# First attention layer of a two-block transformer kernel: token tile 1 ahead of tile 0, share copies ahead of the next scores, and the last output products in another order

## The chip, the cores and the metric

The kernel runs on one core of one Trainium2 chip. The metric is the device time of one execution in microseconds; lower is better. Times of the trace are microseconds from the start of its span.

## The reference, cut to what matters

Two transformer blocks over 256 tokens of width 1024. The part that the change touches is the attention layer of the first block, with the norm behind it:

```
k, v = split(rms_norm(x, kv_norm) @ w_kv)          # 16 heads of 64
q    = rms_norm(x, b_norm) @ w_q
sc   = q_c @ k_c.T * 64**-0.5 + bias[clip(i - j)]  # per chunk of 64 queries, keys of this and the chunks to its left
x    = x + (softmax(sc) @ v) @ w_o
x    = x + (silu(g) * u) @ w_down    with g, u = split(rms_norm(x, ffn_norm) @ w_gate_up)
```

Ahead of it stand a gated mixer and a feed-forward layer; behind it feed-forward 1, and then the second block with its own feed-forwards, sparse and stick-breaking attention and a memory attention.

## The kernel before, in words

The program is written out by hand, engine by engine; the order of the calls in each engine's function is the order in which that engine works, and semaphores join the engines. The 256 tokens are two tiles t of 128 rows.

Every weight matrix is cut into units of 1 MB. SyncE (SP, L562) loads unit u into one of three slots `raw`, once VectorE has split unit u-3. `split_to(n)` on ScalarE (ACT, L730) rounds it into `w_hi` and on VectorE (DVE, L1054) writes the rest into `w_lo`; these are rings of four, so ACT waits until TensorE (PE) has used unit u-4 (`s_used`). `product` (L1663 to L1665) is three matmuls, high by high, high by low and low by high. The units here are `U_KQ` to `U_KQ+7` (keys and queries in turn, 256 columns each), `U_O` to `U_O+3` (output projection) and then, as `U_O+4` and up, gate and up of feed-forward 1.

PSUM holds four accumulators `acc` and four banks `turn`. `take(n)` gives bank n % 4 and waits until VectorE has freed the use before it (`s_tfree`). The numbers are dealt out ahead (`N_S1`, `N_P1`, `T_O`) and must follow the order of the calls on PE and DVE.

The attention runs in six steps (`STEPS1`): for each group g of eight heads, tile 0 with all heads (128 keys) and tile 1 in two steps of four heads (256 keys). A step i is

- `scores(i)` on PE (L1825), into two banks;
- `shift(i)` on DVE: scale and bias (L1209), row maximum (L1212), its negative (L1213), for each half;
- `exps(i)` on ACT (L838): the exponentials, in place in `sc`;
- `turn_shares(i)` on PE (`turn`, L1656): eight transposes into two banks;
- `shares(i)` on DVE: two copies `pt` (L1141);
- `values(i)` on PE (L1845), shares by values, into `acc[2t+1]`.

After the last step of a tile and group come `heads_out(t, g)` on DVE (`xn`, L1229), `turn_heads_out` on PE (four transposes), `high_out` on ACT (L748) and `low_out` on DVE (L1064). `out_tile(t, half, g)` on PE is 12 matmuls of 512 columns of the output projection: eight such tiles, of which (t, half, 0) starts an accumulator and (t, half, 1) ends it. `kq_tile(i, e)` is half a unit of keys or queries, 24 matmuls of 256 columns; `read_kq(i)` on ACT (L829) copies the result to `kt` or `qt`. `read_values(b)` (L821) reads the value block b.

Behind the last output products stand `residual` (L1097), `gained` (`xn`, L1085) and `turn_rows` of the norm, then `by_columns_start`: 48 products of tile 0 of the tokens with the first four gate and up units (i = 0 to 3) and 48 of tile 1, with a hook that turns the second tile's rows ahead of (t=0, i=3).

Of the kernel before, what the change touches and what calls it, by code (L numbers as in the profile page):

```python
# [7 lines left out]
P = 128  # L8
# [4 lines left out]
ACT = mybir.ActivationFunctionType  # L13
# [59 lines left out]
def build(nc, ins, out):  # L73
# [149 lines left out]
    for gp in range(5):  # L223
        if gp < 4:
            MIX_ORDER += [("mix", gp, 0), ("mix", gp, 1)]
        if gp >= 1:
# [15 lines left out]
              for t, js in ((0, (0, 1, 2, 3)), (1, (0, 1)), (1, (2, 3)))]  # L242
    N_S1, N_P1, T_O = [banks(2)], [], {}
    for i in range(6):
        N_P1.append(banks(2))
        if i == 4:
            N_S1.append(banks(2))
            T_O[0, 1] = splits(1)
        elif i < 5:
            N_S1.append(banks(2))  # L250
            if i in (1, 3):
                T_O[(0, 0) if i == 1 else (1, 0)] = splits(1)
        else:
            T_O[1, 1] = splits(1)
# [59 lines left out]
    with ExitStack() as ctx:  # L314
# [405 lines left out]
        def _(act):  # L720
# [104 lines left out]
            def read_kq(i):  # L825

                act.wait_ge(s_used, U_KQ + i + 1)
                dst = (kt_, qt)[i % 2][:, 2 * (i // 2):2 * (i // 2) + 2, :].rearrange("p k n -> p (k n)")
                nc.scalar.activation(dst, acc[2 * (i % 2)][:], ACT.Copy).then_inc(s_kq, 1)  # L829
# [22 lines left out]
            for i in range(4):  # L852
                read_kq(i)
                split_to(U_KQ + 5 + i)
            exps(0)
            read_kq(4)
            split_to(U_O + 1)
            exps(1)
            read_kq(5)
            split_to(U_O + 2)  # L860
            exps(2)
            read_kq(6)
            split_to(U_O + 3)
# [3 lines left out]
            exps(3)  # L867
            exps(4)
            high_out(1, 0)
            exps(5)  # L870
            high_out(0, 1)
            squares(R_FFN1, 0, X, s_row, 3, squares_out[:])
            high_out(1, 1)
            split_to(U_O + 6)
            high_rows(F[1]["norm"], 0, 0)
            split_to(U_O + 7)
            squares(R_FFN1, 1, X, s_read, C_O + 2, squares_out[:])
            split_to(U_O + 8)
            high_rows(F[1]["norm"], 0, 1)
            ffn(1)  # L880
# [158 lines left out]
        def _(dve):  # L1039
# [183 lines left out]
            def heads_out(t, g):  # L1223

                rs = rs1[:, t, 8 * g:8 * g + 8]
                dve.wait_ge(s_exp, 2 * (3 * g + 2 * t + 1))
                link(V.reciprocal(rs, sum1[:, t, 8 * g:8 * g + 8]))
                dve.wait_ge(s_pv, 2 * (3 * g + 2 * t + 1))
# [10 lines left out]
            split_to(U_KQ + 8)  # L1239
            dve.wait_ge(s_rel, 1)  # L1240
            shift(0)
            shares(0)
            shift(1)
            split_to(U_O + 1)
            heads_out(0, 0)
            shares(1)
            shift(2)
            split_to(U_O + 2)
            low_out(0, 0)
            split_to(U_O + 3)  # L1250
            shares(2)
            shift(3)
            heads_out(1, 0)
            split_to(U_O + 4)
            shares(3)
            shift(4)
            low_out(1, 0)
            heads_out(0, 1)
            shares(4)
            shift(5)  # L1260
            low_out(0, 1)
            shares(5)
            residual(2, C_O, U_O + 3, 0)
            heads_out(1, 1)
            gained(G_FFN1, 0, s_row, 3)
            low_out(1, 1)
            split_to(U_O + 6)
            low_rows(F[1]["norm"], 0, 0)
            residual(2, C_O, U_O + 3, 1)
            split_to(U_O + 7)  # L1270
            gained(G_FFN1, 1, s_read, C_O + 2)
            split_to(U_O + 8)
# [371 lines left out]
        def _(pe):  # L1644
# [42 lines left out]
            def by_columns_start(u0, c, src, tr, hooks={}):  # L1687

                for t in range(TT):
                    tok = slice(t * P, (t + 1) * P)  # L1690
                    pe.wait_ge(*freed(tr[t][0] + 1))
                    for i in range(4):
# [7 lines left out]
                        for k in range(4):  # L1700
                            last = product(acc[2 * (b % 2) + t][:], [src(hl, k0 + k)[:, tok] for hl in range(2)],
                                           weights(u, k, BLK), k0 + k == 0, k0 + k == KD - 1)
# [52 lines left out]
            def ffn(f, g, tail, hooks={}):  # L1755
# [7 lines left out]
                by_columns_start(u0, c0, xt_hl(0), F[f]["norm"], {(0, 3): lambda: turn_rows(F[f]["norm"], g, 1), **hooks})  # L1763
# [71 lines left out]
            def values(i):  # L1835
                g, t, js = STEPS1[i]
                nk = keys_of(t)
                if g == 1 and i % 3 < 2:
                    pe.wait_ge(s_o, t + 1)
# [27 lines left out]
            for i in range(4):  # L1867
                if i == 1:
                    pe.wait_ge(*freed(T_Q[1][0] + 1))
                for e in range(2):  # L1870
                    kq_tile(i, e)
            kq_tile(4, 0)
            scores(0)
            kq_tile(4, 1)
            kq_tile(5, 0)
            turn_shares(0)
            scores(1)
            kq_tile(5, 1)
            values(0)
            kq_tile(6, 0)  # L1880
            turn_shares(1)
            scores(2)
            kq_tile(6, 1)
            values(1)
            turn_heads_out(0, 0, 1)
# [411 lines left out]
```

## Time and profile before

| | |
|---|---|
| median of 3 runs | 1272.08 us (1270.84 to 1272.70) |
| the profiled execution, device time | 1273.68 us |
| its span, first to last instruction | 1271.9 us |
| its mean granted TensorE clock | 0.981 of 2.4 GHz |

The span is what the trace sees; 1.8 us of the execution's own time lie around it. Shares of busy time are over the whole span. A timeline row is the start, the duration, the engine, the line, what is written and read and, in brackets, how long the engine had been idle and who released it.

### The profile page before, as it was taken

What the parts mean: (1) busy time and instruction counts of PE and PEld (TensorE: products, weight loads), DVE (VectorE), ACT (ScalarE), POOL (GpSimd) and SP (SyncE); (2) the same over time, 40 slices, a digit from 0 to 9 for tenths busy, and PEclk for the clock granted to TensorE, in tenths of its full rate; (3) what the DMA queues carried; (4) which work ended last, traced back from release to release, by engine and by line L of the source; (5) the groups of instructions that cost most, each with busy time, mean ns of one, the idle gap of its engine ahead of it and who ended that gap; (6) DMA issues with size and microseconds to landing.
All of it is one profiled execution on the core that took longest, in us unless ns stands there. A gap on an engine that the chain in (4) does not pass through costs nothing.

```text
span 1271.9 us, 14904 instructions
## 1 busy us (share of the span) xinstructions
PE 1227.4 (97%) x6231; PEld 1027.6 (81%) x6231; DVE 702.8 (55%) x707; ACT 552.1 (43%) x652; POOL 67.5 (5%) x121
## 2 busy tenths in 40 slices
PE   5998999999999989999998999999999997999998
PEld 4886888888889977888886888888988876888886
DVE  4567356545375655655535555535944677554552
ACT  4444254444355524544524534424555324444341
POOL 4000010000010001010001000003200011000000
PEclk9998999999999979999999999999999897999999
DMA  8752546556486315675554655554752223456550
GB/s 281 254 196 83 196 149 213 184 198 205 160 265 220 112 34 184 199 231 182 207 174 149 198 190 176 205 191 128 230 168 83 84 83 100 155 178 197 199 198 33
DMA packets 147825, 218.46 MB, mean 172 GB/s; under 512 B 5136, under 2 KB 115760, under 8 KB 147632
## 3 DMA queue, kind: packets, MB, share of 16 engines
q1 hardware_dynamic: 144640, 206.69, 49.3%
q0 software_dynamic: 3120, 10.84, 2.6%
q8 instruction: 49, 0.80, 0.3%
q14 instruction: 16, 0.13, 0.0%
HBM read 216.45 MB, written 1.05 MB: 171 GB/s over the span
## 4 chain that ended last, share of the span: by engine, by line
PE 91%; DVE 5%; ACT 1%; issue 1%; DMA 1%; POOL 0%; SPq 0%; DVEq 0%; POOLq 0%; ACTq 0%
PE acc L1663 28%; PE acc L1665 27%; PE acc L1664 27%; PE turn L1656 4%; DVE w_lo L1054 1%; DVE xt L1064 1%; DMA raw<-in_a_w_in 1%; ACT w_hi L730 1%; PE acc L2087 1%; PE turn L2065 1%; PE acc L1845 1%; PE turn L1951 1%; PE turn L1825 1%; DVE pt L1141 0%; PE turn L2036 0%
## 5 line engine op out<-in xcount | busy, mean ns | idle before, releaser
L1054 DVE TENSOR_TENSOR w_lo<-raw,w_hi 128x2048 fp32r<-128x2048 f32 (+1 forms) x196 | 442.4, 2280 | 207.5 <-ACT w_hi L730 207.2
L1663 PE MATMUL acc<-w_hi,xt 128*128 128x512 f32 (+2 forms) x1112 | 438.1, 394 | 13.6 <-DVE xt L1064 9.5
L730 ACT ACTIVATE w_hi<-raw 128x2048 fp32r<-128x2048 f32 (+1 forms) x196 | 368.0, 1906 | 148.4 <-PE acc L1665 117.5
L1665 PE MATMUL acc<-w_hi,xt 128*128 128x512 f32 (+2 forms) x1112 | 430.7, 387 | 0.0
L1664 PE MATMUL acc<-w_lo,xt 128*128 128x512 f32 (+2 forms) x1112 | 430.4, 387 | 0.0
L1663 PEld LDWEIGHTS acc<-w_hi,xt 128*128 128x128 f32 x1112 | 211.5, 190 | 57.8 <-DVE xt L1064 11.8
L1665 PEld LDWEIGHTS acc<-w_hi,xt 128*128 128x128 f32 x1112 | 211.4, 190 | 43.0
L1664 PEld LDWEIGHTS acc<-w_lo,xt 128*128 128x128 f32 x1112 | 211.9, 191 | 40.0
L775 ACT ACTIVATE sg<-acc,rstd 128x256 f32<-128x256 f32 x88 | 37.0, 472 | 246.8 <-PE acc L1665 246.8
L1663 PE MATMUL acc<-w_hi,ht 128*128 128x512 f32 x352 | 139.6, 397 | 0.0
L1665 PE MATMUL acc<-w_hi,ht 128*128 128x512 f32 x352 | 138.0, 392 | 0.0
L1664 PE MATMUL acc<-w_lo,ht 128*128 128x512 f32 x352 | 136.6, 388 | 0.0
L1125 DVE SCALAR_TENSOR_TENSOR hh<-acc,rstd,sg 128x256 f32<-128x256 f32 x88 | 38.5, 479 | 177.1 <-ACT sg L775 177.1
L1665 PEld LDWEIGHTS acc<-w_hi,ht 128*128 128x128 f32 x352 | 66.1, 188 | 15.4
L1664 PEld LDWEIGHTS acc<-w_lo,ht 128*128 128x128 f32 x352 | 66.1, 188 | 14.3
L1663 PEld LDWEIGHTS acc<-w_hi,ht 128*128 128x128 f32 x352 | 66.2, 188 | 12.8
L748 ACT ACTIVATE xt<-turn 128x512 fp32r<-128x512 f32 x54 | 29.7, 597 | 63.5 <-PE turn L1656 63.5
L1663 PE MATMUL acc<-xt,w_hi 128*128 128x256 f32 x192 | 55.1, 287 | 1.3 <-ACT val L821 1.3
L1664 PE MATMUL acc<-xt,w_hi 128*128 128x256 f32 x192 | 54.3, 283 | 0.0
L1665 PE MATMUL acc<-xt,w_lo 128*128 128x256 f32 x192 | 54.3, 283 | 0.0
L615 POOL TENSOR_SCALAR ss<-ss 128x1 f32<-128x1 f32 (+1 forms) x21 | 9.2, 439 | 808.7 <-ACT xn L739 492.6
L1064 DVE TENSOR_TENSOR xt<-turn,xt 128x512 fp32r<-128x512 f32 x54 | 35.0, 685 | 19.2 <-ACT xt L748 18.9
(257 smaller groups left out, 868.8 us busy)
## 6 DMA issues: line engine op xcount, KB each, us to landing
raw<-in_ffn_w_gate_up SPq DMA_DIRECT2D x88, 512.0 KB, 5.1
raw<-in_ffn_w_down SPq DMA_DIRECT2D x22, 1024.0 KB, 5.0
raw<-in_ffn_wg SPq DMA_DIRECT2D x44, 512.0 KB, 4.1
raw<-in_ffn_wu SPq DMA_DIRECT2D x44, 512.0 KB, 5.2
raw<-in_ffn_wd SPq DMA_DIRECT2D x22, 1024.0 KB, 5.1
raw<-in_a_w_in SPq DMA_DIRECT2D x16, 1024.0 KB, 6.0
raw<-in_w_in SPq DMA_DIRECT2D x10, 1024.0 KB, 5.4
raw<-in_a_w_out SPq DMA_DIRECT2D x8, 1024.0 KB, 5.2
```

What stands on the lines that cost most here:

```text
L730: nc.scalar.activation(w_hi[:, u % RING, 0:kt * w], raw[:, u % RAW, 0:kt * w], ACT.Copy).then_inc(s_hi, 1)
L748: nc.scalar.activation(dst, src, ACT.Copy).then_inc(s_thi, 1)
L775: nc.scalar.activation(sg[:, b % 2, t, :], acc[2 * ((c0 + b) % 2) + t][:, 0:FFN_BLK], ACT.Silu, scale=rstd[:, R_FFN[f], t:t + 1]).then_inc ...
L1054: V.tensor_tensor(w_lo[:, u % RING, 0:kt * w], raw[:, u % RAW, 0:kt * w], w_hi[:, u % RING, 0:kt * w].bitcast(F32), ALU.subtract).then_inc ...
L1064: V.tensor_tensor(dst, src, hi.bitcast(F32), ALU.subtract).then_inc(s_tfree, 1)
L1125: last = V.scalar_tensor_tensor(hh[:, b % 2, t, :], acc[2 * ((c0 + b) % 2) + t][:, FFN_BLK:2 * FFN_BLK], rstd[:, R_FFN[f], t:t + 1], sg[:, ...
L1656: last = nc.tensor.transpose(b[:, i * P:(i + 1) * P], src, ident[:])
L1663: mm(o, lhs[0], rhs[0], start=start, stop=False)
L1664: mm(o, lhs[0], rhs[1], start=False, stop=False)
L1665: return mm(o, lhs[1], rhs[0], start=False, stop=stop)
L1825: last = mm(banks2[half][:, e * nk:(e + 1) * nk], qt[rows, j, t * P:(t + 1) * P], kt_[rows, j, 0:nk], start=True, stop=True)
L1845: last = mm(acc[2 * t + 1][:, (h % 8) * HEAD:(h % 8 + 1) * HEAD], pt1[:, half, e * nk + kk * P:e * nk + (kk + 1) * P], val[:, kk, h * HEAD ...
```

## The change

`STEPS1` now has, for each group, tile 1 with its first four heads, tile 1 with its last four, and then tile 0. The accumulators of keys and queries are swapped: the first (keys) is `acc[2]`, so that the first `kq_tile` waits only for value block 0. Scores of step 0 and 3 wait for two reads of keys and queries less, since they need only the first half of a group; step 0 moves up between the halves of `kq_tile` 2. On DVE `shares(i)` stands ahead of `shift(i+1)`, with `shift(4)` and `shift(5)` next to each other. The end is rewritten: which output product stands between which attention parts, `squares` of ACT behind the high copies, and the hook of feed-forward 1 two products later (`late`). The computation is the same.

```
     STEPS1 = [(g, t, [4 * g + j for j in js]) for g in range(2)
-              for t, js in ((0, (0, 1, 2, 3)), (1, (0, 1)), (1, (2, 3)))]
+              for t, js in ((1, (0, 1)), (1, (2, 3)), (0, (0, 1, 2, 3)))]
...
-                        pe.wait_ge(s_read, C_V + 2)
+                        pe.wait_ge(s_read, C_V + 1 + i)
...
-                    last = product(acc[2 * (i % 2)][:, e * TOK:(e + 1) * TOK], weights(u, k, 256, e * P, P),
+                    last = product(acc[2 - 2 * (i % 2)][:, e * TOK:(e + 1) * TOK], weights(u, k, 256, e * P, P),
...
-                pe.wait_ge(s_kq, 4 * (g + 1))
+                pe.wait_ge(s_kq, 4 * (g + 1) - 2 * (i % 3 == 0))
...
-            def out_tile(t, half, g):
+            def out_tile(t, half, g, between=None):
 
                 for k in range(4 * g, 4 * g + 4):
                     u = U_O + k // 2
+                    if k % 4 == 2 and between:
+                        between()
...
-                    if (t, half) == (1, 1 - C_O % 2) and k % 2 == 1:
+                    if (t, half) == (1, C_O % 2) and k % 2 == 1:
                         last.then_inc(s_used, 1)
...
+            kq_tile(2, 0)
+            scores(0)
+            kq_tile(2, 1)
+            kq_tile(3, 0)
+            turn_shares(0)
+            kq_tile(3, 1)
+            values(0)
             kq_tile(4, 0)
-            scores(0)
+            scores(1)
...
             kq_tile(7, 0)
+            turn_shares(3)
+            turn_heads_out(0, 0, 2)
             kq_tile(7, 1)
-            turn_shares(2)
+            values(3)
+            scores(4)
             pe.wait_ge(*freed(T_O[0, 0][0]))
             pe.wait_ge(s_kq, 8)
-            out_tile(0, 0, 0)
-            scores(3)
-            values(2)
-            out_tile(0, 1, 0)
-            turn_shares(3)
-            scores(4)
-            turn_heads_out(1, 0, 2)
-            values(3)
+            near, far = C_O % 2, 1 - C_O % 2
+            out_tile(0, far, 0, lambda: scores(5))
+            out_tile(0, near, 0)
             turn_shares(4)
-            scores(5)
-            turn_heads_out(0, 1, 3)
             values(4)
+            turn_shares(5)
+            pe.wait_ge(s_o, 3)
+            out_tile(1, far, 0)
+            turn_heads_out(1, 1, 3)
+            values(5)
+            pe.wait_ge(*freed(T_O[1, 1][0]))
+            out_tile(1, far, 1, lambda: turn_heads_out(0, 1, 4))
             pe.wait_ge(*freed(T_O[0, 1][0]))
-            out_tile(0, 0, 1)
-            out_tile(0, 1, 1).then_inc(s_half, 1)
-            turn_shares(5)
-            out_tile(1, C_O % 2, 0)
-            values(5)
-            pe.wait_ge(s_o, 4)
-            out_tile(1, 1 - C_O % 2, 0)
-            turn_heads_out(1, 1, 4)
-            pe.wait_ge(*freed(T_O[1, 1][0]))
-            out_tile(1, C_O % 2, 1)
+            out_tile(0, near, 1)
+            out_tile(0, far, 1).then_inc(s_half, 1)
+            out_tile(1, near, 0)
             turn_rows(F[1]["norm"], G_FFN1, 0)
-            out_tile(1, 1 - C_O % 2, 1)
-            ffn(1, G_FFN1, lambda: turn_rows(F[2]["norm"], G_FFN2, 0))
+            out_tile(1, near, 1)
+            ffn(1, G_FFN1, lambda: turn_rows(F[2]["norm"], G_FFN2, 0), late=True)
```

`C_O` is 25, so `near` is half 1 (`acc[0]`, `acc[1]`) and `far` is half 0 (`acc[2]`, `acc[3]`).

What this makes of the order, at two places. On PE before, from the transposes of step 3's shares to the first product of the second group; `sc` are shares, `kt,qt` scores, `xn` head outputs and `val,pt` values:

```order
1908 L1656 MATMUL turn<-ident,sc 128x128 x8
1909 L1825 MATMUL turn<-kt,qt 128x256 x4
1910 L1656 MATMUL turn<-ident,xn 128x128 x4
1911 L1845 MATMUL acc<-val,pt 128x64 x8
1912 L1656 MATMUL turn<-ident,sc 128x128 x8
1913 L1825 MATMUL turn<-kt,qt 128x256 x4
1914 L1656 MATMUL turn<-ident,xn 128x128 x4
1915 L1845 MATMUL acc<-val,pt 128x64 x8
1916 L1663 MATMUL acc<-w_hi,xt 128x512
```

On PE of the change, from `values(3)` to `scores(5)` inside the output tile (its lines stand some numbers lower in the file: L1664 is `turn`, L1836 scores, L1856 values, L1671 to L1673 the product):

```order
1886 L1856 MATMUL acc<-val,pt 128x64 x8
1887 L1836 MATMUL turn<-kt,qt 128x256 x4
1888 L1671 MATMUL acc<-w_hi,xt 128x512
1889 L1672 MATMUL acc<-w_lo,xt 128x512
1890 L1673 MATMUL acc<-w_hi,xt 128x512
1891 L1671 MATMUL acc<-w_hi,xt 128x512
1892 L1672 MATMUL acc<-w_lo,xt 128x512
1893 L1673 MATMUL acc<-w_hi,xt 128x512
1894 L1836 MATMUL turn<-kt,qt 128x128 x8
```

and 18 matmuls of output products later, around `values(4)`:

```order
1913 L1664 MATMUL turn<-ident,sc 128x128 x8
1914 L1856 MATMUL acc<-val,pt 128x64 x8
1915 L1664 MATMUL turn<-ident,sc 128x128 x8
1916 L1671 MATMUL acc<-w_hi,xt 128x512
1917 L1672 MATMUL acc<-w_lo,xt 128x512
```

Before, eight attention groups stand in a row; now both last scores stand ahead of output products, and between two output tiles only three groups are left.

On DVE before, from the shift of step 5 to the norm (`sc` the shift, `pt` the share copies, `X` the residual, `xn<-X` the gain, `xt` the low copies):

```order
157 L1212 TENSOR_REDUCE mx<-sc 128x2
158 L1213 TENSOR_SCALAR nm<-mx 128x2
159 L1064 TENSOR_TENSOR xt<-turn,xt 128x4x128
160 L1141 COPY pt<-turn 128x512 x2
161 L1097 TENSOR_TENSOR X<-acc,X 128x512 x2
162 L1227 RECIPROCAL rs<-sum 128x8
163 L1229 TENSOR_TENSOR xn<-acc,rs 128x512
164 L1085 TENSOR_TENSOR xn<-X,gain_rows 128x1024
165 L1064 TENSOR_TENSOR xt<-turn,xt 128x4x128
166 L1054 TENSOR_TENSOR w_lo<-raw,w_hi 128x2048 x2
167 L1064 TENSOR_TENSOR xt<-turn,xt 128x4x128 x2
```

On DVE of the change, from the copies of step 4 to the low copies of the norm's first tile:

```order
156 L1148 COPY pt<-turn 128x512 x2
157 L1234 RECIPROCAL rs<-sum 128x8
158 L1236 TENSOR_TENSOR xn<-acc,rs 128x512
159 L1148 COPY pt<-turn 128x512 x2
160 L1061 TENSOR_TENSOR w_lo<-raw,w_hi 128x2048
161 L1071 TENSOR_TENSOR xt<-turn,xt 128x4x128
162 L1234 RECIPROCAL rs<-sum 128x8
163 L1236 TENSOR_TENSOR xn<-acc,rs 128x512
164 L1071 TENSOR_TENSOR xt<-turn,xt 128x4x128
165 L1104 TENSOR_TENSOR X<-acc,X 128x512 x2
166 L1092 TENSOR_TENSOR xn<-X,gain_rows 128x1024
167 L1061 TENSOR_TENSOR w_lo<-raw,w_hi 128x2048
```

The weight split of `U_O+3` moved behind the copies of step 5, both head outputs now come ahead of the residual, and one weight split of feed-forward 1 comes ahead of the low copies of the norm.

## Rows read from the trace of the kernel before

**Rows 1.** The page, busy time and share of each engine
```profile
PE 1227.4 (97%) x6231; PEld 1027.6 (81%) x6231; DVE 702.8 (55%) x707; ACT 552.1 (43%) x652; POOL 67.5 (5%) x121
```
**Rows 2.** PE's timeline, the rows of the attention stage behind idle time
```profile
381.93 0.36 PE L1663 MATMUL acc<-xt,w_hi 128*128 128x256 f32 x1 [1.27 <-ACT val L821]
...
449.44 0.63 PE L1656 MATMUL turn<-ident,xn 128*128 128x128 f32 x4 [0.25 <-DVE pt L1141]
...
452.60 0.66 PE L1656 MATMUL turn<-ident,sc 128*128 128x128 f32 x4 [0.79 <-ACT sc L838]
...
454.12 0.92 PE L1656 MATMUL turn<-ident,sc 128*128 128x128 f32 x4 [0.86 <-ACT sc L838]
455.41 2.08 PE L1825 MATMUL turn<-kt,qt 64*128 64x256 f32 x8 [0.38 <-DVE xt L1064]
...
463.01 0.80 PE L1663 MATMUL acc<-w_hi,xt 128*128 128x512 f32 x1 [1.16 <-DVE xt L1064]
...
477.33 0.50 PE L1663 MATMUL acc<-w_hi,xt 128*128 128x512 f32 x1 [0.85 <-DVE xn L1229]
...
482.24 0.50 PE L1663 MATMUL acc<-w_hi,xt 128*128 128x512 f32 x1 [1.41 <-DVE xt L1064]
...
489.05 0.50 PE L1663 MATMUL acc<-w_hi,xt 128*128 128x512 f32 x1 [0.15 <-DVE xt L1064]
```
**Rows 3.** Windows: length, busy time by engine, granted clock (PEclk), DMA share, GB/s
```profile
408.00:448.00 40.00, 40.00 (x325) 37.16 (x324) 28.08 (x40) 21.43 (x58) 0.00 (x0) 1.00 0.34 112
454.40:468.00 13.60, 12.06 (x44) 9.67 (x43) 6.37 (x12) 2.81 (x10) 0.00 (x0) 0.50 0.01 1
...
977.00:982.00 5.00, 5.00 (x45) 4.52 (x44) 2.43 (x6) 0.69 (x1) 0.00 (x0) 1.00 0.02 3
997.00:1007.40 10.40, 10.40 (x51) 9.39 (x51) 6.34 (x12) 3.79 (x9) 0.00 (x0) 0.51 0.58 202
```
**Rows 4.** The chain that ended last: start, duration, engine and line
```profile
408.06 1.09 PE turn L1825 x16
...
415.11 0.87 PE turn L1656 x8
...
420.11 1.73 PE acc L1845 x16
...
431.50 0.44 PE turn L1656 x4
...
487.80 1.21 DVE xt L1064 x2
```
**Rows 5.** PE's timeline: a product behind the norm's transposes, and block 0's end
```profile
498.14 0.47 PE L1663 MATMUL acc<-w_hi,xt 128*128 128x512 f32 x1
...
511.88 0.38 PE L1656 MATMUL turn<-ident,hh 128*128 128x128 f32 x2
```
**Rows 6.** DVE's timeline: shifts, share copies, the splits ahead of feed-forward 1
```profile
409.86 0.68 DVE L1209 SCALAR_TENSOR_TENSOR sc<-turn,rel 128x512 f32<-128x512 f32 x1
...
415.58 1.29 DVE L1141 COPY pt<-turn 128x512 f32<-128x512 f32 x2 [2.60 <-PE turn L1656]
417.08 0.69 DVE L1209 SCALAR_TENSOR_TENSOR sc<-turn,rel 128x512 f32<-128x512 f32 x1 [0.20 <-PE turn L1825]
...
420.04 0.17 DVE L1213 TENSOR_SCALAR nm<-mx 128x2 f32<-128x2 f32 x1
...
483.30 4.50 DVE L1054 TENSOR_TENSOR w_lo<-raw,w_hi 128x2048 fp32r<-128x2048 f32 x2 [1.11 <-ACT w_hi L730]
```
**Rows 7.** ACT's timeline: ends of two steps' exponentials, weights ahead of feed-forward 1
```profile
414.52 0.19 ACT L838 ACTIVATION_READ_ACCUMULATOR sc<-sc,nm 128x1 f32 x1
...
421.15 0.19 ACT L838 ACTIVATION_READ_ACCUMULATOR sc<-sc,nm 128x1 f32 x1
...
481.36 3.71 ACT L730 ACTIVATE w_hi<-raw 128x2048 fp32r<-128x2048 f32 x2
...
492.05 1.92 ACT L730 ACTIVATE w_hi<-raw 128x2048 fp32r<-128x2048 f32 x1 [0.65 <-DMA raw<-in_ffn_w_gate_up]
```

More of the change, by code:

```diff
@@ L241, in build @@
     STEPS1 = [(g, t, [4 * g + j for j in js]) for g in range(2)
-              for t, js in ((0, (0, 1, 2, 3)), (1, (0, 1)), (1, (2, 3)))]
-    N_S1, N_P1, T_O = [banks(2)], [], {}
-    for i in range(6):
+              for t, js in ((1, (0, 1)), (1, (2, 3)), (0, (0, 1, 2, 3)))]
+    N_S1, N_P1, T_O = [], [], {}
+    for i in range(3):
+        N_S1.append(banks(2))
         N_P1.append(banks(2))
[L246 to L254, printed above, removed]
+    N_S1.append(banks(2))
+    T_O[1, 0] = splits(1)
+    N_P1.append(banks(2))
+    T_O[0, 0] = splits(1)
+    for i in (4, 5):
+        N_S1.append(banks(2))
+    for i in (4, 5):
+        N_P1.append(banks(2))
+    T_O[1, 1] = splits(1)
+    T_O[0, 1] = splits(1)
     C_O = blocks(2)
@@ L828, in read_kq @@
                 dst = (kt_, qt)[i % 2][:, 2 * (i // 2):2 * (i // 2) + 2, :].rearrange("p k n -> p (k n)")
-                nc.scalar.activation(dst, acc[2 * (i % 2)][:], ACT.Copy).then_inc(s_kq, 1)
+                nc.scalar.activation(dst, acc[2 - 2 * (i % 2)][:], ACT.Copy).then_inc(s_kq, 1)
             def exps(i):
@@ L851, in _ @@
             split_to(U_KQ + 4)
-            for i in range(4):
-                read_kq(i)
-                split_to(U_KQ + 5 + i)
+            read_kq(0)
+            split_to(U_KQ + 5)
+            read_kq(1)
+            split_to(U_KQ + 6)
             exps(0)
+            read_kq(2)
+            split_to(U_KQ + 7)
+            read_kq(3)
+            split_to(U_KQ + 8)
+            exps(1)
             read_kq(4)
             split_to(U_O + 1)
-            exps(1)
+            exps(2)
             read_kq(5)
             split_to(U_O + 2)
-            exps(2)
+            exps(3)
             read_kq(6)
+            high_out(1, 0)
             split_to(U_O + 3)
@@ L866, in _ @@
             split_to(U_O + 4)
-            exps(3)
             exps(4)
-            high_out(1, 0)
             exps(5)
+            high_out(1, 1)
             high_out(0, 1)
+            split_to(U_O + 5)
+            high_rows(F[1]["norm"], 0, 0)
+            split_to(U_O + 6)
             squares(R_FFN1, 0, X, s_row, 3, squares_out[:])
[L873 to L877, printed above, removed]
             split_to(U_O + 8)
             high_rows(F[1]["norm"], 0, 1)
+            squares(R_FFN1, 1, X, s_read, C_O + 2, squares_out[:])
             ffn(1)
@@ L1242, in _ @@
             shares(0)
+            split_to(U_KQ + 8)
             shift(1)
[L1244 to L1245 removed]
             shares(1)
             shift(2)
[L1248 to L1250 removed]
+            split_to(U_O + 1)
+            heads_out(1, 0)
             shares(2)
             shift(3)
[L1253 removed]
+            split_to(U_O + 2)
+            heads_out(0, 0)
+            low_out(1, 0)
+            shares(3)
+            split_to(U_O + 3)
+            low_out(0, 0)
+            shift(4)
+            shift(5)
+            shares(4)
+            heads_out(1, 1)
+            shares(5)
             split_to(U_O + 4)
[L1255 to L1257 removed]
+            low_out(1, 1)
             heads_out(0, 1)
[L1259 to L1260 removed]
             low_out(0, 1)
[L1262 removed]
             residual(2, C_O, U_O + 3, 0)
[L1264 removed]
             gained(G_FFN1, 0, s_row, 3)
[L1266 removed]
+            split_to(U_O + 5)
+            low_rows(F[1]["norm"], 0, 0)
             split_to(U_O + 6)
[L1268 removed]
             residual(2, C_O, U_O + 3, 1)
[L1270 removed]
+            split_to(U_O + 8)
             gained(G_FFN1, 1, s_read, C_O + 2)
[L1272 removed]
             low_rows(F[1]["norm"], 0, 1)
@@ L1753, in turn_rows, with ffn @@
                     turn(tr[t][0] + q, [xn[:, t, k * P:(k + 1) * P] for k in range(4 * q, 4 * q + 4)])
-            def ffn(f, g, tail, hooks={}):
+            def ffn(f, g, tail, hooks={}, late=False):
                 (u0, ud), c0 = U_FFN[f], F[f]["c"]
@@ L1866, in _ @@
                                                         (1, 2): lambda: [turn_rows(T_Q, G_B, t) for t in range(TT)]})
[L1867 to L1871, printed above, removed]
+            for e in range(2):
+                kq_tile(0, e)
+            pe.wait_ge(*freed(T_Q[1][0] + 1))
+            for e in range(2):
+                kq_tile(1, e)
+            kq_tile(2, 0)
@@ L1872, in _ @@
+            scores(0)
[4 more added lines that the diff above has]
+            values(0)
             kq_tile(4, 0)
-            scores(0)
+            scores(1)
             kq_tile(4, 1)
             kq_tile(5, 0)
[L1876 to L1880, printed above, removed]
             turn_shares(1)
             scores(2)
+            kq_tile(5, 1)
+            values(1)
```

22 lines of the change are left out of this document (14 added, 8 removed).

## The prediction

> **What bounds the kernel now.** I read the page first: PE is busy 1227.4 us of the span [rows 1], so what can be won is PE's idle time and the time that it spends at the lower clock. The waits and then PE's timeline of the attention stage show where it idles [rows 2]: once ahead of the first keys (1.27 us, for ACT's copies of the values), and then eight times between 449 and 489 us: 0.25, 0.79, 0.86, 0.38, 1.16, 0.85, 1.41 and 0.15, together 5.85 us. The releasers are ACT's exponentials and DVE's copies, so what ends last there is a round trip PE, DVE, ACT, DVE, PE with nothing on PE to cover it. The windows show the second loss [rows 3]: up to 448 us PE is busy throughout at a granted clock of 1.00 (2.4 GHz), although scores, transposes and values are mixed into the keys and queries there; from 454.4 to 468.0 it is 0.50 (1.2 GHz), with PE busy 12.06 us. It fell right behind the waits of 0.79 and 0.86 us.
>
> The Trainium skill (TensorE: Matmul & The Clock Gate, "HAM oscillation — how this bites in real kernels") ties the fall to one long idle gap. The trace does not agree: no gap ahead of this fall is longer than 0.86 us. By the page alone I would not count a fall in the new order; below I keep one as a rival.
>
> **What the change gives back.** All amounts of PE work stay: 16 halves of keys and queries at 2.90 us (nine from 381.93 to 408.06 [rows 2, 4]), six scores at 1.09, six transposes of shares at 0.87 to 0.96, six values at 1.73, four transposes of heads at 0.44 [rows 4], eight output tiles at 2.75 (60 matmuls of 512 columns in 511.88 - 498.14 = 13.74 us, so 12 in 2.75 [rows 5]). SP, POOL and the number of DMAs stay too. Only covers change.
>
> 1. *First keys.* `acc[2]` is read out with value block 0, one block ahead of the read that PE waits for, so the 1.27 us come back.
>
> 2. *Exponentials.* From the start of a shift to the end of the exponentials it takes 421.34 - 417.08 = 4.3 us for tile 1 and 414.71 - 409.86 = 4.9 us for tile 0 [rows 6, 7]. Before, step 4's had little more than what stands between 449.44 and 452.60 to hide in [rows 2]. In the new order: step 0's scores end about 1 us before DVE is free of a weight split, so they need 5.3 us and have two key halves, 5.8: 0.5 spare, the thinnest. Steps 1 to 3 have one or two halves, values and transposes: 1.5 to 3.7 spare. Step 4 has an output tile and a half or more plus `scores(5)`: 1.5 + 1.1 + 1.5 + 2.75 = 6.85 against 4.3. Step 5's shift starts behind step 4's, which takes 420.21 - 417.08 = 3.1, so its exponentials end 3.1 + 4.9 = 8.0 us after the scores of 4, and are wanted at 6.85 + 0.95 + 0.45 + 1.75 = 10.0. Both waits (0.79, 0.86) go.
>
> 3. *Head outputs and their low copies.* The way turn, ACT, DVE, PE left PE idle for 1.41 us with nothing on it [rows 2]. Now `values(5)` (1.73) stands behind the turn of (1,1), and half an output tile (1.5) behind the turn of (0,1): both just enough. The 0.85 behind `values(5)` lies under half an output tile; that of `values(4)` under the transposes of step 5 (0.9 against 0.85). The waits 0.25, 0.38, 1.16, 0.85, 1.41 go, within 0.1 each.
>
> 4. *Clock.* With the waits gone PE has an output tile on either side of a stretch of about 4 us (transposes, values, transposes). A like mix held 1.00 from 977 to 982 us with PE busy throughout [rows 3]. If the clock holds, 12.06 us of busy time at half clock become 6.0: 6.0 us back.
>
> 5. *Drains.* A wait costs a little more than its idle row, since the last matmul's end overlaps nothing. I put 0.1 on each of the eight waits, 0.8, an estimate: it is what the walk below gives beyond the other terms.
>
> Back: 1.27 + 5.85 + 6.0 + 0.8 = 13.9 us.
>
> **What it costs.**
>
> a. `values(4)` now directly follows its transposes. The first copy starts 0.47 us behind the first transpose (415.58 against 415.11) and takes half of 1.29, so it ends at 1.12, the second at 1.76 [rows 4, 6]; PE is done with its transposes after 0.87 to 0.96 and waits for the first copy and, if at all, a little for the second: 0.4 us.
>
> b. *Start of feed-forward 1.* `U_O` is released in `out_tile(1, near, 0)`, one product pair into the third tile from the end; PE then has 1.4 + 0.87 + 2.85, about 4.9 us with latencies, left. In that time ACT rounds `U_O+4` (1.86, half of 3.71), DVE splits it (2.25, half of 4.50) and, now behind it, makes the low copies of the norm (1.21) [rows 4, 6, 7]: 5.4. PE waits 0.5, against 0.15 before (already taken as given back). Then the splits of `U_O+5` and `+6` with the residual between them end some 5.7 us after the start, where PE has 5.6 of work: 0.15. `U_O+7` is loaded only when `U_O+4` is split. Before, that split ended at 485.6 and the rounding, released by the DMA, began at 492.05: 6.5 us [rows 6, 7]. So rounding starts 6.5 us behind the split, or 5 if the load alone is quicker; with 1.86 and 2.25 behind it PE waits 0 to 0.95 us. The hook, two products later, leaves 1.4 us of products behind its transposes, for a high copy on ACT and DVE's 1.21 of low copies, some 1.7 to 1.8 from the transposes' end: 0.25 or a little more. Together 0.9 to 1.85; middle 1.4.
>
> c. *Breaks.* Each change from one kind of matmul to products costs about 0.1, an estimate. Two split output tiles and more, smaller pieces among the keys: three breaks more, 0.3.
>
> d. At nothing: `squares` of tile 1 behind the high copies (1.1 us later; its rstd is wanted by the first Silu, 5 us on; without that cover 1.1). `U_O+3` is split behind the copies of step 5; in the walk its product comes 3 us after that, and ACT wants the load behind it 15 us later. In all halves of keys and queries the split is ready over 2 us ahead.
>
> Costs 0.4 + 1.4 + 0.3 = 2.1. Net 13.9 - 2.1 = 11.8 us. As a check I walked PE's new order from 380.6 with these durations: the 48 products of tile 1 end between 499.4 and 500.3 us, against 511.88, so 11.6 to 12.5. From there on the order is as before and PE-bound, so nothing should take it back. The profiled execution's 1273.68 becomes 1261.9; it lies 1.6 above the median of the runs, so the forecast for the median is 1272.08 - 11.8 = 1260.3.
>
> **Rivals.**
>
> *The clock falls again (0.18).* For: it fell behind waits of under a microsecond, and the new tail has one of 0.4 us amid attention groups. Against: before, eight groups in a row and six waits; the stretch at 977. Price: up to the 6.0 of term 4, so 1266.3; half that if it falls for half as long. The Trainium skill (same page, "A second HAM failure mode: psum-queue depth-cycling") says that small idles between groups of matmuls cycling through PSUM banks can make the clock go to and fro, which speaks against an order with more such groups. By it the sum would be this rival's; the trace agrees for 454 us and not for 408 to 448.
>
> *Thin covers fail (0.11).* Step 0's exponentials, the low copies, the splits of feed-forward 1: three places with under 0.5 us spare, each late by a microsecond: 1263.3.
>
> *The waits only move (0.04).* Every wait on DVE turns up at the next consumer, and the clock falls as before: 1271, within 0.2%.
>
> *Slower (0.05).* Scores and values now start 13 us earlier (395 instead of 408), so more of the stage is a mix. If PE went to 1.2 GHz in it early and stayed there, it would cost half of that time: 23.6 us at 1.2 GHz undo the 11.8; 30 us give 1275.5. For: falls last long here (13.6 us; 10.4 at 997 us [rows 3]). Against: the same mix held 1.00 for the 40 us up to 448 us.
>
> **How the numbers follow.** The forecast case has 0.62, with a range of its own of 1258.3 to 1262.5: the bounds of b (0.5 each way), the drains (0.8), and the low stretches further on, which may begin or end a little otherwise when everything ahead of them is 12 us earlier (10.4 us at half clock is worth 5; I allow 1.5 either way). The range of 8 in 10 reaches up over both middle rivals to 1266.5; below there is no more to win than the 0.9 to 1.85 of b, so 1258.0. Faster by over 0.2% (2.5 us, about what a measurement of this kernel can tell): 0.91; within it 0.04; slower 0.05.
>
> **What the changed profile would show.** PE's first key product without idle ahead of it; the granted clock 1.00 from 381 to 500 us; no row of PE waiting for ACT's `sc`; one wait of about 0.4 us for `pt` around 452; one of about 0.5 us at the first gate and up product around 476, and perhaps one for `w_lo` at 484; the first `hh` transpose near 500 instead of 511.88; the rest of the trace shifted by 12 us. I am wrong if the clock shows 0.50 around 450 to 465, if PE waits for `sc` around 402, or if the gain at 500 us is given back later.

## The result, and the profile after

The changed kernel takes 1260.64 us (median of 4 runs, 1259.60 to 1262.52) against 1272.22 us (4 runs, 1270.84 to 1272.70): a ratio of 0.9911 with a 95% interval of 0.9899 to 0.9924, 11.6 us faster. The forecast was 1260.3. The profiled execution took 1260.18 us, with a span of 1258.5 us and a mean granted clock of 0.989. Two executions far outside all the others, 2049.05 us for the kernel before and 2442.75 us for a variant further down, are left out of what follows.

The page's first line for the changed kernel: PE has the same 6231 matmuls and is 7.3 us less busy than in [rows 1]; the other engines are as before.

```profile
PE 1220.1 (97%) x6231; PEld 1022.9 (81%) x6231; DVE 702.5 (56%) x707; ACT 551.9 (44%) x652; POOL 66.9 (5%) x121
```

PE's timeline, with the last 16 transposes ahead of the stage, the change from the last value product to the first key product, all the rows with idle time between 379 and 499 us, two product rows around a wait of the weight loads, and the first transpose of feed-forward 1:

```profile
372.26 1.91 PE L1664 MATMUL turn<-ident,xn 128*128 128x128 f32 x16
...
379.24 0.39 PE L1673 MATMUL acc<-w_hi,xt 128*128 128x512 f32 x1
379.46 0.28 PE L1671 MATMUL acc<-xt,w_hi 128*128 128x256 f32 x1
...
451.44 2.00 PE L1856 MATMUL acc<-val,pt 128*128 128x64 f32 x16 [0.41 <-DVE pt L1148]
...
475.49 0.51 PE L1671 MATMUL acc<-w_hi,xt 128*128 128x512 f32 x1 [0.46 <-DVE xt L1071]
...
483.72 0.39 PE L1673 MATMUL acc<-w_hi,xt 128*128 128x512 f32 x1
484.22 0.51 PE L1671 MATMUL acc<-w_hi,xt 128*128 128x512 f32 x1
...
488.35 0.50 PE L1671 MATMUL acc<-w_hi,xt 128*128 128x512 f32 x1 [0.18 <-DVE xt L1071]
...
499.36 0.60 PE L1664 MATMUL turn<-ident,hh 128*128 128x128 f32 x4
```

Products of 512 columns otherwise start 0.23 us apart; the two at 483.72 and 484.22 are 0.50 apart, since the second waits for `w_lo`.

Nine waits [rows 2] have become three. The first key product follows the last value product at once; no row waits for ACT's `sc`. The windows of the changed kernel (length; PE, PEld, DVE, ACT and POOL busy; granted clock; DMA share; GB/s), first those that answer to [rows 3], then everything ahead of the stage, the stage from the 16 transposes to the first `hh` transpose, and everything behind it:

```profile
408.00:448.00 40.00, 40.00 (x332) 37.19 (x332) 28.38 (x44) 20.32 (x51) 0.00 (x0) 1.00 0.36 120
454.40:468.00 13.60, 13.58 (x71) 11.20 (x72) 5.42 (x7) 1.20 (x2) 0.00 (x0) 1.00 0.25 77
...
0.00:372.26 372.26, 355.30 (x1596) 293.43 (x1597) 201.47 (x174) 158.80 (x146) 26.59 (x52) 0.99 0.59 198
372.26:499.36 127.10, 125.91 (x857) 111.89 (x856) 79.87 (x94) 64.45 (x113) 7.04 (x10) 1.00 0.48 154
499.36:1258.50 759.14, 738.91 (x3780) 617.56 (x3778) 421.12 (x441) 328.68 (x393) 33.26 (x59) 0.99 0.50 165
```

The same three parts of the kernel before:

```profile
0.00:373.30 373.30, 355.88 (x1597) 293.24 (x1597) 201.57 (x174) 158.83 (x146) 27.37 (x52) 0.99 0.59 197
373.30:511.88 138.58, 131.45 (x858) 116.59 (x857) 79.91 (x94) 64.48 (x113) 7.01 (x10) 0.95 0.44 142
511.88:1271.90 760.02, 740.07 (x3780) 617.81 (x3778) 421.29 (x441) 328.81 (x393) 33.11 (x59) 0.98 0.50 165
```

The stage went from 138.58 to 127.10 us, 11.48 less; that is nearly all of the 11.6 us between the medians. The two profiled spans differ by 13.4: 1.04 more ahead of the stage and 0.88 more behind it, where the program is the same. Those parts vary from one execution to the next (behind the stage 756.9 to 761.5 us over the kernels below, with low-clock stretches of other lengths), so from here on I read the stage's length. It tells kernels apart that the whole time does not.

### The profile page after: what moved, and what is told of

It reads as the page before. It is cut to its first block, busy times and chain, and to the rows that moved or that the text cites. A ratio compares the mean times of both kernels' runs of the same rounds, so it can differ in the third digit from the quotient of the medians.

```text
span 1258.5 us, 14904 instructions
## 1 busy us (share of the span) xinstructions
PE 1220.1 (97%) x6231; PEld 1022.9 (81%) x6231; DVE 702.5 (56%) x707; ACT 551.9 (44%) x652; POOL 66.9 (5%) x121
## 4 chain that ended last, share of the span: by engine, by line
PE 91%; DVE 4%; ACT 2%; DMA 1%; issue 1%; POOL 0%; SPq 0%; DVEq 0%; ACTq 0%; POOLq 0%
PE acc L1671 28%; PE acc L1673 27%; PE acc L1672 27%; PE turn L1664 4%; DVE w_lo L1061 1%; ACT w_hi L732 1%; PE acc L1856 1%; PE acc L2103 1%; DVE xt L1071 1%; DMA raw<-in_a_w_in 1%; PE turn L2081 1%; PE turn L1967 1%; PE turn L1836 1%; DMA raw<-in_ffn_w_gate_up 0%; PE turn L1986 0%
## 5 line engine op out<-in xcount | busy, mean ns | idle before, releaser
L1671 PE MATMUL acc<-w_hi,xt 128*128 128x512 f32 (+2 forms) x1112 | 438.0, 394 | 10.5 <-DVE xt L1071 6.8
L1673 PE MATMUL acc<-w_hi,xt 128*128 128x512 f32 (+2 forms) x1112 | 430.3, 387 | 0.0
L1671 PEld LDWEIGHTS acc<-w_hi,xt 128*128 128x128 f32 x1112 | 211.3, 190 | 55.5 <-DVE xt L1071 9.5
L1673 PEld LDWEIGHTS acc<-w_hi,xt 128*128 128x128 f32 x1112 | 210.8, 190 | 42.8
L1671 PE MATMUL acc<-w_hi,ht 128*128 128x512 f32 x352 | 139.7, 397 | 0.0
L1673 PE MATMUL acc<-w_hi,ht 128*128 128x512 f32 x352 | 138.1, 392 | 0.0
L1673 PEld LDWEIGHTS acc<-w_hi,ht 128*128 128x128 f32 x352 | 66.1, 188 | 15.4
L1671 PEld LDWEIGHTS acc<-w_hi,ht 128*128 128x128 f32 x352 | 66.3, 188 | 12.8
L1671 PE MATMUL acc<-xt,w_hi 128*128 128x256 f32 x192 | 55.5, 289 | 0.0
L1673 PE MATMUL acc<-xt,w_lo 128*128 128x256 f32 x192 | 54.3, 283 | 0.0
L1071 DVE TENSOR_TENSOR xt<-turn,xt 128x512 fp32r<-128x512 f32 x54 | 35.0, 684 | 13.5 <-ACT xt L750 13.4
```

The lines of the kernel that those rows point to most:

```text
L1071: V.tensor_tensor(dst, src, hi.bitcast(F32), ALU.subtract).then_inc(s_tfree, 1)
L1671: mm(o, lhs[0], rhs[0], start=start, stop=False)
L1673: return mm(o, lhs[1], rhs[0], start=False, stop=stop)
```

## Experiments

In all of them "stage" is the time from the 16 transposes to the first `hh` transpose: 138.58 us before, 127.10 changed. Kernels are compared with runs of the kernel before on the same chip.

### The accumulators of keys and queries as before

```diff
-   acc[2 - 2 * (i % 2)][:], ACT.Copy)
+   acc[2 * (i % 2)][:], ACT.Copy)
...
-   pe.wait_ge(s_read, C_V + 1 + i)
+   pe.wait_ge(s_read, C_V + 2)
```

The same swap of `acc` stands in `product`. 

> The changed kernel with only the swap of the key and query accumulators undone (keys in acc[0], first key product behind both value reads). If the first-keys term stands by itself, PE idles 1.3 us again ahead of the first key product and the time is 1.3 us above the changed kernel's 1260.6: about 1261.9. If the wait was hidden by something further on, it stays at 1260.6.

Measured: 1265.11 us, ratio 0.9945 (0.9932 to 0.9959), stage 129.14. PE's timeline has the old wait back, to the hundredth:

```profile
381.51 0.36 PE L1671 MATMUL acc<-xt,w_hi 128*128 128x256 f32 x1 [1.27 <-ACT val L823]
```

The stage lost 2.04 us, not 1.3; the rest is a wait of 0.66 us for `w_lo` in feed-forward 1, of which more below. The time is 3.2 us above the expected 1261.9, and 4.5 above the changed kernel's median, more than the stage shows. Its profiled execution was one of its faster ones (1263.26 us; all six lie between 1263.22 and 1267.81): of the 3.0 us between its span (1261.5) and that of the changed kernel, 2.04 lie in the stage and the rest where the program is the same. What the median has beyond that, no trace shows.

### The new steps, but the output products in a row at the end

```diff
-   out_tile(0, far, 0, lambda: scores(5))
-   out_tile(0, near, 0)
+   scores(5)
    turn_shares(4)
    values(4)
    turn_shares(5)
-   out_tile(1, far, 0)
    turn_heads_out(1, 1, 3)
    values(5)
-   out_tile(1, far, 1, lambda: turn_heads_out(0, 1, 4))
+   turn_heads_out(0, 1, 4)
+   out_tile(0, far, 0); out_tile(0, near, 0)
+   out_tile(1, far, 0); out_tile(1, far, 1)
```

The waits between these calls are left out of the diff; the order on DVE and ACT is that of the changed kernel.

> The changed kernel with the output products of group 0 taken out from between the last attention parts: scores 5, shares 4, values 4, shares 5, values 5 and both head transposes stand in a row behind scores 4, and the output tiles follow. Step order, first keys, DVE and ACT stay as changed. If the output products are the cover, PE waits about 3.3 us for step 4's exponentials, about 1 us for its copies, and some more; 4 to 5 us of idle in all, and the clock falls behind it as before, 3 to 6 us more: 1268 to 1271. If idle alone counts and the clock holds: 1265. If the order of the steps alone gives the gain, products or no products between: 1261.

Measured: 1271.23 us, ratio 0.9995 (0.9984 to 1.0005), stage 137.48. All but 1.1 us of the stage's gain is gone. The first keys' wait is still absent, which alone is worth about that much. The tail in PE's timeline:

```profile
446.07 0.66 PE L1664 MATMUL turn<-ident,sc 128*128 128x128 f32 x4 [1.94 <-ACT sc L840]
447.59 0.66 PE L1664 MATMUL turn<-ident,sc 128*128 128x128 f32 x4 [0.86 <-ACT sc L840]
450.09 3.67 PE L1856 MATMUL acc<-val,pt 128*128 128x64 f32 x16 [1.85 <-DVE pt L1148]
...
459.96 1.11 PE L1664 MATMUL turn<-ident,xn 128*128 128x128 f32 x4 [1.95 <-DVE xn L1236]
```

The values of step 4 last 3.67 us, those of the changed kernel 2.00: the clock fell, as the windows of the same kernel say.

```profile
449.30:456.10 6.80, 6.01 (x28) 6.01 (x29) 3.35 (x7) 1.85 (x10) 0.00 (x0) 0.50 0.00 0
459.50:462.90 3.40, 2.94 (x9) 2.55 (x10) 1.10 (x2) 0.60 (x1) 0.00 (x0) 0.50 0.95 298
```

So the order of the steps and the copies ahead of the next scores, as they stand, win nothing further without the output products between them.

### One cover moved: `scores(5)` behind both output tiles

```diff
-   out_tile(0, far, 0, lambda: scores(5))
+   out_tile(0, far, 0)
    out_tile(0, near, 0)
+   scores(5)
```

> The changed kernel with scores 5 behind the two output tiles of token tile 0 instead of inside the first. Shift 5 starts some 4 us later, so the exponentials of step 5 end 1.5 to 2.5 us after PE wants them. Cover theory: that idle and no more if the clock holds: 1262.5; with a fall of the clock behind the wait up to 6 us on top, 1264 to 1268.5. Rival: the place of scores 5 doesn't matter, 1260.6.

Measured: 1267.12 us, ratio 0.9961 (0.9948 to 0.9973), stage 133.30, that is 6.2 us lost by moving 1.1 us of work. Up to the first gate and up product the stage lost 5.26 us (481.37 - 372.88 = 108.49 against 475.49 - 372.26 = 103.23); the other 0.94 lie behind it, where this trace has a wait of 1.02 us for `w_lo`. PE's timeline, and the windows of the same kernel:

```profile
454.35 3.68 PE L1856 MATMUL acc<-val,pt 128*128 128x64 f32 x16 [2.80 <-DVE pt L1148]
```

```profile
449.00:454.40 5.40, 2.60 (x27) 1.89 (x26) 3.70 (x8) 2.18 (x11) 0.00 (x0) 1.00 0.01 3
454.40:461.20 6.80, 6.80 (x28) 6.46 (x29) 3.34 (x6) 1.00 (x6) 0.00 (x0) 0.50 0.00 0
```

It was one wait, for `pt` and not for `sc` as I had expected: the copies of step 4 now stand on DVE behind the shift of step 5, which stands behind the late scores. The wait grew from 0.41 to 2.80, and with it the clock fell for 6.8 us.

### The same with PE kept at work in the wait

Nine more matmuls of 512 columns go into a free bank ahead of `values(4)`, and are overwritten there; the output is unchanged.

```diff
    scores(5)
    turn_shares(4)
+   for _ in range(9):
+       mm(take(N_P1[5])[:], xt[0][:, 0, 0, 0:P], w_hi[:, U_O % RING, 0:BLK], start=True, stop=True)
```

> The kernel with scores 5 late, with nine extra matmuls of 512 columns in its wait of 2.80 us ahead of values 4; they are overwritten, no output changes. That kernel's stage was 133.3 us, 6.2 above the changed one's, with the clock at 0.50 for 6.8 us. If the wait makes the clock fall, it now holds 1.00 and the stage is 129.9 to 130.5: the wait alone costs 2.4 to 3, the clock 3 to 3.4. If the clock falls for another reason, the stage stays at 133.3 or grows.

Measured: 1265.34 us, ratio 0.9938 (0.9922 to 0.9954), stage 129.78. PE's timeline, and the window of the same kernel that fell before:

```profile
450.51 2.33 PE L1920 MATMUL turn<-w_hi,xt 128*128 128x512 f32 x9
453.55 2.00 PE L1856 MATMUL acc<-val,pt 128*128 128x64 f32 x16 [0.71 <-DVE pt L1148]
```

```profile
454.40:461.20 6.80, 6.80 (x49) 6.00 (x49) 4.72 (x6) 0.81 (x3) 0.00 (x0) 1.00 0.02 5
```

The clock stayed at 1.00, and 3.5 of the 6.2 us came back (133.30 - 129.78). The order on DVE and the moment when `pt` is ready are the same; only PE was at work meanwhile. The wait for `w_lo` also differs between the traces (1.02 us late, 0.51 here), so I part the loss where it hasn't entered yet, at the first gate and up product: 477.60 - 372.08 = 105.52. Of the 5.26 us, 2.97 (108.49 - 105.52) go with the clock and 2.29 (105.52 - 103.23) with the wait, which had grown by 2.39.

### The clock alone in the kernel before

The same kind of matmuls go into the kernel before: three ahead of each wait for the exponentials of step 4, and in a second kernel another twelve behind `values(4)`.

```diff
    for half in range(2):
+       if i == 4:
+           for _ in range(3):
+               mm(take(N_P1[i] + half)[:], xt[0][:, 0, 0, 0:P], w_hi[:, U_O % RING, 0:BLK], start=True, stop=True)
        pe.wait_ge(s_exp, 2 * i + half + 1)
```

> The kernel before, with three extra matmuls of 512 columns ahead of each of the two waits for step 4's exponentials (their results are overwritten by the transposes; no output changes). They stand where PE idled 0.79 and 0.86 us, so by themselves they cost next to nothing. If the clock fell at 454.4 us because PE idled there, it now holds 1.00 or falls later and for less: up to 6 us less, 1266. If it falls because scores, transposes and values follow each other with waits further on, or whatever PE does, it stays within 1 us of 1272.2.

Measured with the six: 1272.15 us, ratio 0.9995 (0.9987 to 1.0004), stage 138.47. Its windows and the row of its timeline that answers to the 1.16 in [rows 2]:

```profile
454.40:460.70 6.30, 3.50 (x28) 3.02 (x28) 5.22 (x11) 1.96 (x7) 0.00 (x0) 1.00 0.01 3
460.70:467.50 6.80, 5.32 (x13) 4.16 (x14) 0.69 (x1) 0.70 (x3) 0.00 (x0) 0.50 0.00 0
```

```profile
462.18 0.79 PE L1663 MATMUL acc<-w_hi,xt 128*128 128x512 f32 x1 [3.52 <-DVE xt L1064]
```

Half of the slow stretch is gone and 0.1 us is won, since PE only reached the next wait earlier: it went from 1.16 to 3.52. The chain over DVE and ACT set the time there, and the slow matmuls lay inside it. So the clock did what the theory said (a later fall, for less), while the time came out where the text had put the rival that idle has nothing to do with it: by the time alone one would have drawn the wrong conclusion.

> The kernel before with extra matmuls of 512 columns in all the long waits of the tail: three ahead of each half of step 4's shares, as in the first filling, and twelve behind values 4, where PE then idled 3.52 us ahead of the first output tile of group 1. They are overwritten; no output changes. If idle makes the clock fall, it now stays at 1.00 up to 480 us and the 24 products behind that wait run in 5.5 us instead of 7.9: 2.4 us less, about 1269.5. If the path up to there is the round trip of DVE and ACT, nothing more than that is won, since idle takes the place of slow work. Rival, that the whole 6.0 us of the clock term come back: 1266. If the clock falls for all that: 1272.

Measured with all eighteen: 1270.46 us, ratio 0.9983 (0.9974 to 0.9991), stage 135.95. The window where [rows 3] has 0.50:

```profile
454.40:468.00 13.60, 11.96 (x67) 9.61 (x66) 6.28 (x12) 2.85 (x10) 0.00 (x0) 1.00 0.00 1
```

The full clock alone is worth 2.6 us of the stage in the kernel before, against the 6.0 of term 4. The waits left in this tail (0.25, 0.17, 0.64, 0.30, 0.70, 0.85 and 1.41 us) did not bring a fall. Nor did 0.85 and 1.41 in the kernel before [rows 2], as its window shows:

```profile
476.00:489.00 13.00, 10.63 (x53) 8.27 (x52) 8.22 (x8) 6.66 (x6) 0.25 (x1) 1.00 0.17 47
```

So the length of a single wait does not tell whether the clock falls.

### The first keys alone in the kernel before

The swap of `acc[0]` and `acc[2]`, with its wait, and nothing else. 

> The kernel before with only the swap of the key and query accumulators. First-keys term alone: PE's idle of 1.27 us ahead of the first key product is gone, 1.3 to 1.4 us less than before, ratio 0.9989. Rival, that the swap is worth 3 to 4 us, as the keys-back kernel read: 0.997. Rival, hidden further on: 1.000.

Measured: 1271.01 us, ratio 0.9991 (0.9983 to 1.0000), stage 137.35, so 1.23 less. The row with 1.27 is gone from PE's timeline. The clock's low stretch came out differently in this trace, in two parts:

```profile
452.30:455.70 3.40, 3.02 (x13) 2.29 (x14) 3.14 (x7) 0.00 (x0) 0.00 (x0) 0.51 0.02 5
459.20:466.00 6.80, 5.73 (x14) 4.47 (x15) 0.69 (x1) 0.29 (x1) 0.00 (x0) 0.50 0.00 0
```

That is 10.2 us at half clock instead of 13.6, and it did not shorten the stage: the wait ahead of the first output product of the second group is 2.69 us here against 1.16 in [rows 2]. It is the same finding as with the six extra matmuls.

### The tail of the changed kernel

The changed kernel once more, on the chip of the variant that follows. 

> The changed kernel once more, on the same chip and beside the same runs of the kernel before as the three kernels that follow, as their yardstick. Theory: 0.9911 of the kernel before, 1260.7 us. If the keys-back kernel's distance (0.9945) was a matter of the chip and not of the 1.3 us wait, this one lies near 0.993 to 0.995 here.

Measured: 1262.43 us, ratio 0.9924 (0.9912 to 0.9937), stage 128.09. The ratio lies between the theory's 0.9911 and the 0.993 that would have spoken for the chip, so it doesn't decide. The 0.99 us on the first run's stage are one row of PE's timeline. In the first run that wait cost PE about 0.3 us, the 0.50 instead of 0.23 us between two products:

```profile
487.26 0.50 PE L1671 MATMUL acc<-w_hi,xt 128*128 128x512 f32 x1 [1.07 <-DVE w_lo L1061]
```

`U_O+7` is loaded only when `U_O+4` has been split, so this wait varies with the DMA (from the end of that split to the rounding it took 5.4 to 6.6 us in the traces of the changed kernel and its variants). In the changed kernel's first trace the split (first row) ended at 474.24 and the rounding began 5.7 us later, released by the DMA:

```profile
471.95 2.29 DVE L1061 TENSOR_TENSOR w_lo<-raw,w_hi 128x2048 fp32r<-128x2048 f32 x1 [0.82 <-ACT w_hi L732]
...
479.92 1.92 ACT L732 ACTIVATE w_hi<-raw 128x2048 fp32r<-128x2048 f32 x1 [2.32 <-DMA raw<-in_ffn_w_gate_up]
```

Three variants of the tail followed. The shares of step 4 turned in the middle of the second output tile:

```diff
-   out_tile(0, near, 0)
-   turn_shares(4)
+   out_tile(0, near, 0, lambda: turn_shares(4))
```

> The changed kernel with the transposes of step 4's shares between the two unit halves of the near output tile of token tile 0 instead of behind it. Their exponentials end at 447.5 and they would stand at 448.6; DVE is free at 449.4 and copies until 450.7, when PE reaches values 4 at 450.9. Cover theory: PE's idle of 0.41 us goes, one break of 0.1 comes: 0.3 us less than the changed kernel, 1260.3, which only the trace can tell. Rival: the copies aren't the wait, and the idle stays.

Measured: 1260.39 us (5 runs), ratio 0.9909 (0.9895 to 0.9923), stage 127.14. The 0.41 us row is gone. Up to the first gate and up product the stage is 0.69 us shorter (475.12 - 372.58 = 102.54 against 103.23), against 0.3 expected; a `w_lo` wait of 0.85 behind that takes it back.

The hook of feed-forward 1 where it stood before (no `late`):

> The changed kernel with late=False: the transposes of the norm's second tile stand ahead of the fourth gate and up unit again, not two products into it. In the changed kernel's trace that unit starts at 484.4 and the gained rows end at 485.3, so PE waits 0.9 us for them; the 0.2 us at the second tile's start go. Theory: stage 0.5 us longer, not to be told from 1260.6 by time. Rival: the place of the hook is free: no idle row for xn.

Measured: 1262.87 us, ratio 0.9924 (0.9907 to 0.9941), stage 127.41, with the wait that the text expected; the kernel before, whose gain ends earlier against these transposes, has none there:

```profile
487.21 1.09 PE L1664 MATMUL turn<-ident,xn 128*128 128x128 f32 x8 [0.95 <-DVE xn L1092]
```

So `late` trades this wait for the one on `w_lo` behind it; in the stage there is nothing between them that a single trace could tell.

On DVE the gain of the norm's second tile ahead of the split of `U_O+7` instead of behind it (`split_to(n)` splits the units below n), and the hook early:

```diff
-   split_to(U_O + 8)
+   split_to(U_O + 7)
    gained(G_FFN1, 1, s_read, C_O + 2)
+   split_to(U_O + 8)
    low_rows(F[1]["norm"], 0, 1)
```

> The changed kernel with DVE's gain of the second tile ahead of its split of U_O+7, while that unit's load is still under way, and the hook back ahead of the fourth unit, so that the transposes cover the split. The gain costs DVE at most 0.4 us ahead of the split; PE loses the waits for w_lo (0 to 1.07 us in the two traces) and for the low copies (0.2). Theory: 0.3 to 1 us less than the changed kernel. Rival: the later split costs as much as the cover gives: same.

Measured: 1261.47 us, ratio 0.9914 (0.9899 to 0.9928), stage 126.38. Neither the wait for `w_lo` nor that for `xn` is in its trace. The last kernel has both, this and the earlier turn:

> The changed kernel with both edits, step 4's transposes inside the near output tile and the gain first with the early hook. Theory: the amounts add, 0.3 to 0.4 and 0.3 to 1: stage of 126.5 us from the transposes ahead of the last value products to the first of the hidden rows, against 127.1 to 128.1, and some 0.9900 of the kernel before. Rival: no more than turn4_early alone (0.9909).

Measured: 1259.99 us, ratio 0.9906 (0.9890 to 0.9923), stage 125.88. One row with idle time is left in the stage:

```profile
475.05 0.50 PE L1672 MATMUL acc<-w_hi,xt 128*128 128x512 f32 x1 [0.47 <-DVE xt L1071]
```

Its stage is 1.2 to 2.2 us shorter than that of the changed kernel in its two traces, and both parts are there: 102.57 us up to the first gate and up product (103.23 and 103.25 changed) and 23.31 behind it (23.87 and 24.84; 23.15 with the gain first alone). The ratios (0.9906 against 0.9911 and 0.9924, and 0.9909 for the rival) don't tell them apart.

## Why the prediction was right, and which term was off

It ended at 0.3 us from the median. By its steps:

- **Term 1, first keys.** Forecast 1.27. The group ahead of the keys fell from 381.93 - 373.30 = 8.63 [rows 2] to 379.46 - 372.26 = 7.20 us, 1.43 less. Alone in the kernel before it gave 1.23 in the stage, and undone in the changed kernel the 1.27 was back. Right.
- **Terms 2 and 3, the round trips.** The eight waits, 5.85 us, are gone as announced, and what is left are the waits that stand among the costs. The spare time at step 0, the thinnest, came out at 0.8 us against 0.5: its exponentials end at 400.07 and are turned at 400.87. With the output products moved out, waits of 1.94, 0.86, 1.85 and 1.95 us were back, so these covers do the work that the text gave them. Moving one cover of 1.1 us brought a wait of 2.8 back, though by the order on DVE and not by the exponentials, a path that this term did not have.
- **Term 4, the clock.** It held 1.00 throughout, as forecast. That the fall hung on what PE does in the waits is shown from both sides: in the kernel before it stayed away with PE given other work, and in the changed one it came back with one wait and went again with other work in that wait. The extra matmuls are themselves products of 512 columns, so these runs don't part idle time from a lack of wide products. For idle time speaks that the kernel with all eighteen has no wide product for 4.9 us behind the sixth (454.15 to 459.05), with waits of 0.17, 0.64 and 0.30 us, and held 1.00, while with scores 5 late it fell 5.0 us behind the last product, with PE busy 2.2 us of them. That is an argument from two traces; no run parts the two causes. As a term of its own, though, 6.0 us holds only beside terms 2 and 3. In the kernel before the full clock alone was worth 2.6 us, since much of the slow work lay under the chain over DVE and ACT. The sum came near because the change took both; read alone, the step "12.06 us of busy time at half clock become 6.0" is too much. The Trainium skill (TensorE: Matmul & The Clock Gate, "A second HAM failure mode: psum-queue depth-cycling") describes a kernel that cycles through PSUM banks with small idles between groups of matmuls and whose clock goes to and fro. The output products in a row look like that, with waits of up to 1.95 us and the clock at 0.50, 1.00 and 0.50 again. The changed kernel cycles through the same four banks with three waits of up to 0.46 us and has 1.00 over 127.10 us, so the cycling without the idles was not enough.
- **Term 5, drains.** Forecast 0.8. No run shows it by itself. PE's busy time in the stage fell by 5.54 us (131.45 to 125.91). Terms 4 and 5 less cost c had 6.0 + 0.8 - 0.3 = 6.5 for that, so together they were 1.0 too high.
- **Costs a and b.** Forecast 0.4 and 1.4. Measured on PE: 0.41 at the values of step 4, 0.46 at the first gate and up product (forecast 0.5 at 476, found at 475.49), 0.18 at the second tile (0.25), and about 0.3 for `w_lo`: 1.35 against 1.8. The bounds of 0 to 0.95 for `w_lo` were near: up to 1.07 over the traces. PE's idle time in the stage fell from 138.58 - 131.45 = 7.13 to 127.10 - 125.91 = 1.19 us, 5.94 less, where the sum had 1.27 + 5.85 - 1.8 = 5.3.
- **Cost c, breaks.** Forecast 0.3. The groups of keys and queries, with all that lies up to the next group, took 0.36 us more in total.

So the mechanism held, and the closeness is in part luck: idle time gave 0.6 us more than forecast, busy time 1.0 less, and together the stage has 11.48 us against 11.8. Two slips in the text touch nothing: 30 us at 1.2 GHz give 1260.3 + 15 = 1275.3 and not 1275.5, and the eight groups in a row had five waits [rows 2], not six.

From the first key product to the first `hh` transpose the time went from 129.95 to 119.90 us, 10.05 less. Summed by kind of PE work, each group up to the start of the next, that is: values 4.83 less, transposes of heads and norm 2.20, share transposes 1.35, scores 1.25, products of 512 columns 0.78, keys and queries 0.36 more.

The rivals: the clock did not fall with the announced 0.4 us wait, but with 2.80 us in its place it did; the clock's part of that loss was 3.0 us, as the rival priced a fall of half the length (6.8 us here, 13.6 before). No thin cover failed: the three waits left are those that stand among the costs. The clock did not fall early in the longer mix either, which was the way to a slower kernel. The waits that only move are what the output products in a row show: 1271.23 us for a rival at 1271. Nothing of the gain was given back behind the stage.

What stays open, beside that about the clock: DVE's copies ahead of the next shift were not tried alone, because the bank numbers tie them to the order of the steps. So how much of the tail's gain needs them as well isn't known; the output products in a row show only that they don't give it by themselves.

## What to carry to other kernels

Where several short waits lie in a row on the engine that bounds the kernel, look at what that engine could do meanwhile, and compare each cover with the whole round trip that it must hide: a microsecond of work in the wrong place cost over 5 us here, more than half of it by the clock behind the wait. To price a fallen clock, don't halve the busy time alone; ask which of the slow work lies under a chain of other engines, or keep the clock up with dummy matmuls and measure. And where the change touches a tenth of the program, read the length of that stage from the traces: it showed steps of a microsecond that the whole time could not.

## What the runs showed of the hardware

- Eighteen dummy matmuls of 512 columns kept the granted clock at 1.00 through a tail that without them had 0.50 for 13.6 us; nine did so in the changed kernel with its scores late (0.50 for 6.8 us without).
- Waits of 0.25, 0.79 and 0.86 us [rows 2] preceded a fall; waits of 0.41 or 0.71 us did not, and neither did 0.85 and 1.41 us between output products. In the kernel whose output products stand in a row, the clock was 0.50 for 6.8 us, back, and 0.50 again for 3.4 us.
- The clock's low stretches elsewhere are not the same in two executions of the same instructions. Near 17.5 us the kernel before had one of 3.4 us and the changed kernel none, with the same program up to there. The identical part behind the stage took 756.9 to 761.5 us over the traces, so a whole time can move by a microsecond or two with nothing changed.
